# Experts' gather and scatter as rounded-format matmuls on high and low parts, gates applied at the copy out of PSUM

## The reference

```python
h2 = modulate(rmsnorm(x_lat, norm2_g), sh2, sc2)      # 256 tokens x 1024
# router: one group of 4 experts by argmax, in it the top 2 of 4 experts,
# gates[e, t] = softmax weight of token t for expert e (0 for the 14 others)
for e in range(16):                                   # EXPERT_HIDDEN = 512
    y = (silu(h2 @ w1[e]) * (h2 @ w3[e])) @ w2[e]
    acc = acc + gates[e][:, None] * y
x_lat = x_lat + g2 * acc                              # then a last rms norm
```

## Time and profile before

| | before |
|---|---|
| median of 3 runs | 1125.32 us (1122.8 to 1128.25) |
| profiled execution, its own time | 1122.61 us |
| its span | 1120.8 us |
| TensorE busy | 91% of the span |
| VectorE, ScalarE, GpSimd busy | 43%, 36%, 35% |
| mean granted TensorE clock | 0.961 |
| read from HBM | 244.59 MB, 219 GB/s over the span |

### The profile page before, as it was taken

The page is one execution under the profiler, slowest core; times in us unless marked ns, Lnnn a source line. Parts: engine busy times, 40 slices in busy tenths (PEclk is TensorE's granted clock), DMA queues, the critical chain, the costliest instruction groups (busy, mean ns, idle before and its releaser), DMA issues.

```text
span 1120.8 us, 13844 instructions
## 1 busy us (share of the span) xinstructions
PE 1022.1 (91%) x5577; PEld 745.7 (67%) x5577; DVE 480.6 (43%) x628; ACT 408.7 (36%) x600; POOL 389.7 (35%) x191
## 2 busy tenths in 40 slices
PE   3998799967999999998899989996989999999994
PEld 3997687745899988987698856664766434444331
DVE  4468322371355435545407417774454122222224
ACT  4444754512554344333454425553233211111001
POOL 4579573833730000002587834446640000000000
PEclk9999899998899999998899999998998999999997
DMA  9545342655665665756254532235687799999960
GB/s 319 189 148 186 112 159 73 218 186 208 199 205 177 237 225 159 261 183 224 80 184 150 188 99 89 75 113 186 253 300 295 298 421 421 422 420 422 420 256 39
DMA packets 84515, 246.60 MB, mean 220 GB/s; under 512 B 4388, under 2 KB 8123, under 8 KB 72031
## 3 DMA queue, kind: packets, MB, share of 16 engines
q1 hardware_dynamic: 82766, 240.47, 58.8%
q0 software_dynamic: 1264, 2.41, 0.9%
q10 hardware_dynamic: 416, 2.77, 0.6%
HBM read 244.59 MB, written 1.05 MB: 219 GB/s over the span
## 4 chain that ended last, share of the span: by engine, by line
PE 80%; DVE 9%; ACT 4%; issue 2%; DMA 2%; POOL 2%; SPq 0%; POOLq 0%; ACTq 0%; DVEq 0%
PE gemm_ps L1217 10%; PE gemm_ps L758 8%; PE gemm_ps L759 7%; PE gemm_ps L760 7%; PE gemm_ps L762 7%; PE gemm_ps L764 7%; PE gemm_ps L763 7%; PE gemm_ps L1248 5%; PE mix_ps L1258 2%; PE gemm_ps L1201 2%; PE mix_ps L758 2%; PE mix_ps L759 2%; PE mix_ps L760 2%; PE gemm_ps L936 1%; DMA ring<-in_w_out_dram 1%
## 5 line engine op out<-in xcount | busy, mean ns | idle before, releaser
L442 POOL TENSOR_TENSOR w_lo<-ring,w_hi 128x1024 fp32r<-128x1024 f32 (+1 forms) x144 | 360.1, 2523 | 423.0 <-ACT w_hi L436 422.9
L436 ACT ACTIVATE w_hi<-ring 128x1024 fp32r<-128x1024 f32 (+2 forms) x222 | 227.2, 1035 | 295.8 <-PE gemm_ps L764 97.1
L758 PE MATMUL gemm_ps<-w_hi,acts 128*128 128x512 f32 (+2 forms) x448 | 179.3, 400 | 27.1 <-POOL w_lo L442 10.4
L762 PE MATMUL gemm_ps<-acts,w_hi 128*128 128x256 f32 x640 | 184.9, 289 | 3.8 <-DVE acts L1729 2.4
L764 PE MATMUL gemm_ps<-acts,w_lo 128*128 128x256 f32 x640 | 181.8, 284 | 0.0
L763 PE MATMUL gemm_ps<-acts,w_hi 128*128 128x256 f32 x640 | 181.7, 284 | 0.0
L759 PE MATMUL gemm_ps<-w_lo,acts 128*128 128x512 f32 (+2 forms) x448 | 174.4, 389 | 0.0
L760 PE MATMUL gemm_ps<-w_hi,acts 128*128 128x512 f32 (+2 forms) x448 | 173.8, 388 | 0.0
L442 DVE TENSOR_TENSOR w_lo<-ring,w_hi 128x1024 fp32r<-128x1024 f32 (+1 forms) x78 | 90.7, 1170 | 107.5 <-ACT w_hi L436 107.3
L762 PEld LDWEIGHTS gemm_ps<-acts,w_hi 128*128 128x128 f32 x640 | 123.5, 193 | 9.3 <-issue 6.5
L763 PEld LDWEIGHTS gemm_ps<-acts,w_hi 128*128 128x128 f32 x640 | 123.5, 193 | 1.3 <-issue 1.2
(11 more groups left out here) (347 smaller groups left out, 1423.9 us busy)
## 6 DMA issues: line engine op xcount, KB each, us to landing
ring<-in_w_in_dram SPq DMA_DIRECT2D x56, 1024.0 KB, 5.2
ring<-in_w_mod_dram SPq DMA_DIRECT2D x24, 1024.0 KB, 5.2
ring<-in_w_ffn_in_dram SPq DMA_DIRECT2D x20, 1024.0 KB, 5.2
late_ring<-in_w_exp_down_dram SPq DMA_DIRECT2D x20, 1024.0 KB, 12.4
late_ring<-in_w_exp_gate_dram SPq DMA_DIRECT2D x18, 1024.0 KB, 12.7
late_ring<-in_w_exp_up_dram SPq DMA_DIRECT2D x18, 1024.0 KB, 10.5
ring<-in_w_ffn_out_dram SPq DMA_DIRECT2D x11, 1024.0 KB, 9.4
ring<-in_w_exp_up_dram SPq DMA_DIRECT2D x9, 1024.0 KB, 11.5
```

The lines of the kernel that those rows point to most:

```text
L436: nc.scalar.activation(part(w_hi, u), raw_unit(u), ACT.Copy).then_inc(hi_made, 1)
L442: eng.tensor_tensor(part(w_lo, u), raw_unit(u), part(w_hi, u), ALU.subtract).then_inc(lo_made[unit["maker"]], 1)
L758: mm(dst, xh, wh, start=a_, stop=False, skip_group_check=True)
L762: mm(dst, wh, xh, start=a_, stop=False, skip_group_check=True)
```

## The change: what it does

- **Gather.** The normed tokens are kept as a rounded high part `XH` (ScalarE, in place of `XN3`) and a low part `x_low` = exact - `XH` (four new VectorE instructions of 128x512). `PICK` becomes fp32r, and each f32 matmul becomes two fp32r matmuls. For the first group the high ones go before `mod_spread`, the low ones behind it.
- **Scatter.** `PICK_T` holds plain ones and zeros. The gates become `SLOT_GATES`, one factor for each slot: four f32 matmuls of 2 columns for each group (`slot_gates`), copied by VectorE. ScalarE writes the high part of gate x y (two instructions of 64x512), VectorE then the low part (two more), both out of `DOWN`. Each f32 scatter matmul becomes two fp32r ones; both halves of the tokens are scattered in the odd steps, none in the even ones.
- **Gone:** `pick_gates` and its wait. `PICK` has three buffers in place of two, `PICK_T` and `YS` one in place of two. Some semaphores of the weight slots are shared.

```diff
-                for i in range(2):
-                    k = 2 * q + i
-                    for t in range(TT):
-                        last = mm(dst[...], XN3[:, t, k * P:(k + 1) * P], PICK[:, g % 2, t, :], ...)
+                for v in parts:                      # parts=(XH, x_low)
+                    for i in range(2):
+                        k = 2 * q + i
+                        for t in range(TT):
+                            last = mm(dst[...], v[:, t, k * P:(k + 1) * P], PICK[:, g % 3, t, :], ...)
...
             def pick_turn(p):
-                pe.wait_ge(sem("picked_gates"), p + 1)
...
+            def slot_gates(g):
+                pe.wait_ge(sem("picked"), g + 1)
+                pe.wait_ge(sem("gates"), TT)
+                for pair in range(2):
+                    e = PER_GROUP * g + 2 * pair
+                    for t in range(TT):
+                        last = mm(TURNED[:, SEQ + e:SEQ + e + 2], PICK_F[:, g % 3, t, pair * P:(pair + 1) * P], GATES[:, t, e:e + 2], ...)
+                last.then_inc(sem("slot_gates"), 1)
...
             def scatter(p, t):
-                pe.wait_ge(sem("y_by_scalar"), 2 * p + 2)
-                pe.wait_ge(sem("y_by_vector"), 2 * p + 2)
+                pe.wait_ge(sem("y_low"), 4 * p + 4)
                 for half in range(2):
-                    last = mm(PM[:, 2 * t + half, :], PICK_T[:, p % 2, t * P:(t + 1) * P], YS[:, p % 2, half, :], ...)
+                    for part_ in range(2):
+                        last = mm(PM[:, 2 * t + half, :], PICK_T[:, t * P:(t + 1) * P], YS[:, part_, half, :], ...)
...
+            pe.wait_ge(sem("x4_rows"), 2)
             for q in range(4):
-                gather(0, q)
+                if q == 2:
+                    pe.wait_ge(sem("totals_read"), 1)
+                gather(0, q, (XH,))
             mod_spread("mod_g2", 1)
+            for q in range(4):
+                pe.wait_ge(sem("x_low"), 2 * (q // 2 + 1))
+                gather(0, q, (x_low,))
             for s in range(NEXP + 1):
...
+                if s < NEXP and s % PER_GROUP == 0:
+                    slot_gates(s // PER_GROUP)
...
-                if s >= 3:
-                    scatter((s - 3) // 2, (s + 1) % 2)
+                if s >= 3 and s % 2 == 1:
+                    for t in range(TT):
+                        scatter((s - 3) // 2, t)
...
# ScalarE, after down_product
-                    A(YS[r:r + WIN, p % 2, 0, :], DOWN[0:WIN, :], ACT.Copy).then_inc(sem("y_by_scalar"), 1)
+                    for half in range(2):
+                        b = slice(half * WIN, (half + 1) * WIN)
+                        A(YS[r:r + WIN, 0, half, :], DOWN[b, :], ACT.Copy, scale=SLOT_GATES[r:r + WIN, e:e + 1]).then_inc(sem("y_high"), 1)
# VectorE, before the router's totals are read
+            for half in range(2):
+                own = slice(half * COL, (half + 1) * COL)
+                for t in range(TT):
+                    V_.scalar_tensor_tensor(x_low[:, t, own].rearrange(...), x[:, t, own].rearrange("q (p k) -> q k p", k=4),
+                                            x4_r[:, t:t + 1], XH[:, t, own].rearrange(...), ALU.mult, ALU.subtract).then_inc(sem("x_low"), 1)
# VectorE, after down_product
-                    V_.tensor_copy(YS[rows_, p % 2, 1, :], DOWN[WIN:P, :]).then_inc(sem("y_by_vector"), 1)
-                if s % 2 == 1:
-                    pick_gates(s // 2)
+                    for half in range(2):
+                        dve.wait_ge(sem("y_high"), 2 * e + half + 1)
+                        V_.scalar_tensor_tensor(YS[rows_, 1, half, :], DOWN[half * WIN:(half + 1) * WIN, :], SLOT_GATES[rows_, e:e + 1],
+                                                YS[rows_, 0, half, :], ALU.mult, ALU.subtract).then_inc(sem("y_low"), 1)
```

More of the change, by code:

```diff
@@ L402, in late_raw @@
             return v.rearrange("p (k n) -> p k n", k=k)
[L404 to L405 removed]
+        in_ring = [len([i for i in range(len(pieces)) if i % RING == r]) for r in range(RING)]
+        late_landed = [sem(f"late_landed{slot}") for slot in range(LATE_RING - RING)] + landed
+        landed_earlier = [0] * (LATE_RING - RING) + in_ring
+        first_landed = [sem("ws_in"), sem("vec_rows")]
+        first_earlier = [1, len(ROWS)]
         def late_wait(eng, f):
             if f < FIRST:
[L409 removed]
+                eng.wait_ge(first_landed[f], 16 * (first_earlier[f] + 1))
             else:
[L411 removed]
+                slot = (f - FIRST) % LATE_RING
+                eng.wait_ge(late_landed[slot], 16 * (landed_earlier[slot] + (f - FIRST) // LATE_RING + 1))
         late_used = sem("late_used")
@@ L1188, in _, with gather @@
             mod_rows("mod_g2", 1, KT // 2, KT)
-            def gather(g, q):
+            def gather(g, q, parts=(XH, x_low)):
                 pe.wait_ge(sem("picked"), g + 1)
[L1193 to L1196, removed]
                 dst = gathered_to(g, q)
-                for i in range(2):
-                    k = 2 * q + i
-                    for t in range(TT):
-                        last = mm(dst[:, i * GROUP_SLOTS:(i + 1) * GROUP_SLOTS], XN3[:, t, k * P:(k + 1) * P], PICK[:, g % 2, t, :],
-                                  start=(t == 0), stop=(t == TT - 1))
-                last.then_inc(sem("gathered"), 1)
+                for v in parts:
+                    for i in range(2):
+                        k = 2 * q + i
+                        for t in range(TT):
+                            last = mm(dst[:, i * GROUP_SLOTS:(i + 1) * GROUP_SLOTS], v[:, t, k * P:(k + 1) * P], PICK[:, g % 3, t, :],
+                                      start=(v is XH and i == 0 and t == 0), stop=(v is x_low and t == TT - 1), skip_group_check=True)
+                if parts[-1] is x_low:
+                    last.then_inc(sem("gathered"), 1)
             def gate_and_up(e):
@@ L1295, in _ @@
             with pe.If(again == 1):
+                pe.wait_ge(sem("rest_rows"), 1)
                 for k in range(KT):
```

86 lines of the change are left out of this document (49 added, 37 removed).

## The result

| | before | after |
|---|---|---|
| median | 1125.68 us (6 runs, 1122.8 to 1128.25) | 1115.26 us (6 runs, 1112.79 to 1117.81) |
| ratio, 95% interval | | 0.9908 (0.9892 to 0.9923) |
| profiled execution (span) | 1122.61 us (1120.8) | 1112.79 us (1111.0) |
| router's first small product to the end, in the profile | 260.5 us | 252.4 us |
| mean granted clock | 0.961 | 0.958 |

The kernel became 10.4 us faster; 13.5 had been forecast. The two profiles differ by 9.8 us, and 1.7 of that lie ahead of the router, in code that the change doesn't touch: its first small product starts at 860.34 before and 858.62 after.

What follows compares the result with a forecast made beforehand. TensorE's instructions were taken as the bound, neck and neck with the weight stream. Terms: 1.4 + 2.3 + 3.8 + 5.7 + 1.5 - 3.6 + 2.8 - 0.45 = 13.5 us, so 1125.3 becomes 1112; range 1104 to 1119.

Steps and rivals of the forecast that it cites:

- the gather's 0.77 a step: Gather in steps 0 to 11: eight fp32r matmuls at 0.96 us in place of four f32 at 1.73.
- the slot gates at 0.11 an instruction: Four groups of 8 new TensorE instructions: 0.9 us a group, 3.6 us lost in all, at most 7.7.
- the wait for ScalarE in even steps: Without scatter as cover, TensorE idles about 1.2 us before the down product until ScalarE has copied the gather.
- the forecast's own branch of 11.5 to 16: Whole kernel: the outcome that 11.5 to 16 us are gained, given chance 0.57.
- the weights bind: Rival: a weight stream 1% slower makes TensorE wait in steps 14 and 15; gain 11, so 1114 us; chance 0.13.
- 1.0 for the last down product alone: Last step: 1.0 us lost to a down product partly at half clock, range 0 to 1.7.
- the 0.9 said for its faster form: Tail: first half of the last scatter 0.9 us less, against copies costing 1.4 more.
- One sign of being wrong: Trace after: DMA waits earlier, granted clock falling inside the loop, or even steps' down product over 3 us after gate and up.
- The rival of the falling clock: Waits bring half-clock stretches of 1.7 us each; eight eat the gain, fourteen make it 1136 us; chance 0.05.
- the bounds: Start: four `x_low` take 2.8 to 5.6 us, saving 2.6 or 0.1 us; the middle, 1.4, was taken.
- The spread: Start, between the high and low gather matmuls: high done at 869.1, spread at 871.1.
- the margin of 2.9 us: Step 15: the gate product's second two weight pieces needed at 1073.5 land by 1070.6, so the stream just allows 13.5 us.

Runs made afterwards that it cites:

- kept_busy: Changed kernel with matmuls whose results nobody reads put into TensorE's waits in step 12, the last step and before the last scatter; ratio to before 0.9925.
- totals_first: Changed kernel with VectorE reading the router's totals before it makes the four low parts of x; ratio to before 0.9905, router to end 247.2 us.
- scatter_part: The change without the gather's part: f32 gather as before, scatter in the rounded format with slot gates and both copies; ratio to before 1.0016.
- slot_in_gap: Changed kernel with the slot gates' eight small products moved behind the hidden transposes, where TensorE waits for the gather's copy; router to end 249.2 us.
- combined: Changed kernel with totals read first, slot gates in the wait, and unread matmuls in the late waits; ratio to before 0.9868, router to end 244.25 us.
- gather_best: Kernel before with the gather's part alone, totals read first, and gated pick matrices made ahead of the down product's copy; ratio to before 0.984.
- gather_part: Kernel before with only the gather's part of the change; scatter, gates and copies as before; ratio to before 0.9944.
- after_again: Changed kernel, unchanged, as a control on another chip; ratio to before 0.9948, router to end 252.3 us.

## Why the prediction was right or wrong

**Right: the bound and the step.** TensorE's own order set the time; the gather's 0.77 a step (0.80 in steps 1 and 2) and the slot gates at 0.11 an instruction came as worked out, and the wait for ScalarE in even steps came where it was said, with 0.9 us for 1.2. Steps 0 to 11 gained 9.0 for 9.1 said. Inside, two misses cancel: the scatter's matmuls are 0.25 apart and not 0.228 (0.2 more in each odd step), and the even steps needed 2.48, not 2.61.

The whole gain, 10.4 us, lies inside the stated range of times but below the forecast's own branch of 11.5 to 16, and from the router on, in the profiles, it is 8.1. The median of 1115 is close to the 1114 of the rival "the weights bind", by coincidence: in the changed kernel no wait for weights appears.

**Wrong in size: the clock.** The step that failed is the price put on the granted clock: 1.0 for the last down product alone. It fell at step 12 too (1.7 us, in both profiles of the changed kernel), took the full 1.7 at the last down product, and kept the last scatter slow, so that the 0.9 said for its faster form did not come. kept_busy gets 4.2 of it back. One sign of being wrong was a clock that falls inside the loop, and it did, in step 12. The rival of the falling clock was true at two places, not at fourteen: single waits of 0.9 us in the loop left it alone, two of them close together had it fall in both profiles of the changed kernel and not in those of totals_first and scatter_part, whose step 12 has the same waits.

**Wrong in size: the start.** Four `x_low` at 1.06 us are just the middle between the bounds (2.8 to 5.6 for all), but the stage gained 0.3 and not 1.4. Up to the end of the high matmuls the prediction's chain held: the totals came at router + 8.1 and the high matmuls ended at + 10.0, as its own figures have it for 4.2 us of `x_low` (8.2 and 10.2). The spread is what was mis-sized: 2.88 us from its start to the low matmuls, partly at half clock, in place of 2.0. The two bounds were also not worked out alike: by the steps of the first, the second ends at 875.8 and not at 875.4, so that the middle was 1.1 or 1.2 and not 1.4. `x_low` at its stride has a mean of 1.125 us for 512 elements, the same instruction in line out of PSUM on 64 partitions 0.75. The rule of the Trainium skill (SBUF — State Buffer, section Door 1: The DMA port swizzle, the note on cachelines) goes the same way on VectorE, with a factor of 1.5 and not the 2 of ScalarE's rows; the two VectorE rows differ in memory and partitions as well, so the factor isn't the stride's alone.

**Copies.** 0.68 and 0.75 in place of 0.59 and 0.69; from the last down product's end to the scatter 2.35 us. Hidden in the loop, as said.

**The weight stream** did not bind, as said, but the margin of 2.9 us was too large, and here there was luck. By the prediction's arithmetic (pieces start again when the first gate product ends, 199.3 us to the last, the pieces of the second half of gate product 15 four pieces before it) they would be there at router + 211.3 in slot_in_gap and + 208.5 in combined; TensorE went on at 213.8 and 210.4, 2 to 2.5 us later. That leaves under 1 us of the 2.9. The changed kernel kept clear of it because it gained 8.1 us before step 15 and not 11.1. What the arithmetic lacks is open.

**Not seen at all:** that the forecast's own terms already gave the gather 9.2 and the scatter's part, slot gates, steps 12 to 14, last step and tail the other 4.3 together. I added them up and never set them against each other by part of the change. scatter_part (no gain, 1.0016) and gather_best (as fast as combined without it) show it: the scatter in the rounded format gains nothing here over its slot gates and its second copy.

**Open:** what makes the part ahead of the router start 858 to 869 us in. It is in no code changed here, and may make up much of the spread of the times, but no kernel has profiles of both a short and a long execution. The longer executions of a kernel show the lower mean clock (kept_busy: 0.963 or 0.964 for its four shortest, 0.952 for its longest), and gather_part's profile, at 0.947, lost 3.9 us to half clock behind the router's first product as well.

## What to carry to other kernels

Add up a change's terms by its parts, and not only by its stages: a part whose saved matmul time was also the cover of a copy can be worth nothing. When matmuls get cheaper beside a full weight stream, work out at once at which step the stream binds, and what must follow its last piece in series; that sets the floor. And look whether a new instruction on another engine stands ahead of something small that TensorE waits for: moving one reduction brought the first gate product 2.8 to 3.3 us forward in three profiles, where the whole change gave 8.1.

## What the runs showed of the hardware that was not expected

- Two waits of TensorE of 0.78 and 0.86 us, 0.4 us of work between them, were followed by a granted clock of 0.65 and a down product of 5.35 in place of 3.65 us in two profiles, and by full clock in two others (totals_first, scatter_part). Waits of 2.52 and 0.52 us before the last down product were followed by 5.11 to 5.35 us in after, after_again, totals_first and slot_in_gap; with unread matmuls in them the granted clock was 1.00 and the product took 3.65 (kept_busy).
- The scatter's eight fp32r matmuls of 512 columns take 2.02 us, 0.25 each, where those of the large products are 0.22 to 0.23 apart.
- A wait in the middle of a gate product appears as "issue" of the weight loads (2.01 us in combined), with no transfer named; that it is a wait for weights is inferred. At the start of the same product in slot_in_gap the weight load's row says "issue" (1.59) and the matmul's row names the DMA (0.74). The table of steps shows both.
